# Three VectorE steps moved ahead of dE in a delta rule woven into a weight stream, and a 480-byte pad taken out

## The reference

```
proj = rms_norm(x) @ even_w_in        # attention A | qkv of B | gate z | beta, a
qkv  = silu(causal_conv(qkv_b));  q, k = l2_norm(q), l2_norm(k)
beta = sigmoid(beta_raw);  g = -exp(a_log) * softplus(a_raw + dt_bias)
# gated delta rule, 8 heads of 128, in chunks:
decay = exp(gam_i - gam_j) for i >= j             # gam = cumsum(g)
A     = I + strict_lower(beta_i * (k_i . k_j) * decay)
u, w  = solve(A, [v * beta, k * beta * exp(gam)])
v_new = u - w S
o     = (q exp(gam)) S + (q . k * decay, lower incl.) v_new
S     = S exp(gam_last) + (k exp(gam_last - gam))^T v_new
out_b = o * rsqrt(mean(o*o) + eps) * onorm * silu(z)
h     = x + concat(attention, out_b) @ even_w_out
```

## Time and profile before

| | |
|---|---|
| median of 3 runs | 2695.59 us (2693.42 to 2699.34) |
| the profiled execution, its time | 2695.59 us |
| its span, first to last instruction | 2693.8 us |
| TensorE busy | 2654.5 us, 99% |
| VectorE busy | 1548.3 us, 57% |
| ScalarE busy | 1263.1 us, 47% |
| mean granted TensorE clock | 0.998 of full |

### The profile page before, as it was taken

The page is one execution under the profiler, slowest core; times in us unless marked ns, Lnnn a source line. Parts: engine busy times, 40 slices in busy tenths (PEclk is TensorE's granted clock), DMA queues, the critical chain, the costliest instruction groups (busy, mean ns, idle before and its releaser), DMA issues.

```text
span 2693.8 us, 35362 instructions
## 1 busy us (share of the span) xinstructions
PE 2654.5 (99%) x12523; PEld 2206.6 (82%) x12523; DVE 1548.3 (57%) x2553; ACT 1263.1 (47%) x2381; POOL 28.6 (1%) x34
## 2 busy tenths in 40 slices
PE   8999999999999999999999999999999999999998
PEld 7778877888888888888788888888888888888876
DVE  6877756655555555555555555555555555565656
ACT  6552244544444444444555544444444444445433
POOL 1000000000000000000000000000000000000000
PEclk9999999999999999999999999999999999999999
DMA  7552223666565656557555656565656665565664
GB/s 220 176 161 86 66 92 110 194 181 196 185 194 187 190 187 193 190 193 227 165 171 188 198 181 198 182 195 186 194 186 192 192 190 155 172 180 171 178 233 158
DMA packets 251152, 477.47 MB, mean 177 GB/s; under 512 B 19080, under 2 KB 22912, under 8 KB 250400
## 3 DMA queue, kind: packets, MB, share of 16 engines
q1 hardware_dynamic: 245808, 467.92, 55.7%
q10 hardware_dynamic: 4656, 7.15, 0.7%
q0 software_dynamic: 576, 0.90, 0.1%
HBM read 473.82 MB, written 2.10 MB: 177 GB/s over the span
## 4 chain that ended last, share of the span: by engine, by line
PE 91%; DVE 6%; ACT 1%; issue 1%; DMA 0%; ACTq 0%; SPq 0%; POOL 0%; DVEq 0%
PE ps L1025 28%; PE ps L1027 28%; PE ps L1026 28%; PE ps L809 2%; DVE gs L1241 1%; DVE w_lo L1516 1%; PE ps L1088 1%; PE ps L1087 1%; ACT w_hi L711 0%; PE ps L1078 0%; DVE gs L1239 0%; PE ps L1167 0%; PE ps L1011 0%; PE ps L1009 0%; PE ps L1010 0%
## 5 line engine op out<-in xcount | busy, mean ns | idle before, releaser
L1516 DVE TENSOR_TENSOR w_lo<-raw,w_hi 128x512 fp32r<-128x512 f32 (+1 forms) x1776 | 1154.5, 686 | 745.9 <-ACT w_hi L711 743.2
L711 ACT CAST w_hi<-raw 128x512 fp32r<-128x512 f32 (+1 forms) x1776 | 1032.3, 622 | 708.9 <-PE ps L1027 567.8
L1025 PE MATMUL ps<-w_hi,xh 128*128 128x512 f32 (+1 forms) x2464 | 971.8, 394 | 7.8 <-DVE w_lo L1516 6.9
L1027 PE MATMUL ps<-w_hi,xl 128*128 128x512 f32 (+1 forms) x2464 | 957.5, 389 | 0.0
L1026 PE MATMUL ps<-w_lo,xh 128*128 128x512 f32 (+1 forms) x2464 | 956.4, 388 | 0.0
L1025 PEld LDWEIGHTS ps<-w_hi,xh 128*128 128x128 f32 x2464 | 463.4, 188 | 105.4 <-DVE w_lo L1516 15.4
L1027 PEld LDWEIGHTS ps<-w_hi,xl 128*128 128x128 f32 x2464 | 463.0, 188 | 96.6
L1026 PEld LDWEIGHTS ps<-w_lo,xh 128*128 128x128 f32 x2464 | 463.7, 188 | 90.0
L1025 PE MATMUL ps<-w_hi,fh 128*128 128x512 f32 x1056 | 416.3, 394 | 5.7 <-DVE w_lo L1516 5.7
L1027 PE MATMUL ps<-w_hi,fl 128*128 128x512 f32 x1056 | 412.4, 391 | 0.0
L1026 PE MATMUL ps<-w_lo,fh 128*128 128x512 f32 x1056 | 412.1, 390 | 0.0
(11 more groups left out here) (292 smaller groups left out, 1105.9 us busy)
## 6 DMA issues: line engine op xcount, KB each, us to landing
raw<-in_ffn_w_gate SPq DMA_DIRECT2D x176, 512.0 KB, 4.5
raw<-in_ffn_w_up SPq DMA_DIRECT2D x176, 512.0 KB, 4.6
raw<-in_ffn_w_down SPq DMA_DIRECT2D x176, 512.0 KB, 4.3
raw<-in_w_in SPq DMA_DIRECT2D x112, 512.0 KB, 4.1
raw<-in_even_w_in SPq DMA_DIRECT2D x80, 512.0 KB, 3.7
raw<-in_odd_w_in SPq DMA_DIRECT2D x64, 512.0 KB, 4.4
raw<-in_even_w_out SPq DMA_DIRECT2D x32, 512.0 KB, 3.8
raw<-in_odd_w_out SPq DMA_DIRECT2D x32, 512.0 KB, 4.6
```

The source lines that it names most:

```text
L711: act.copy(w_tile(w_hi, w2_hi, blk, k), raw[:, slot, kk, 0:blk.width]).then_inc(hi_ready, 1)
L1025: pe.matmul(acc(blk, t), hi_x[:, blk.kt0 + k, tok], hi_w, start=(k == 0), stop=False)
L1027: ins = pe.matmul(acc(blk, t), lo_x[:, blk.kt0 + k, tok], hi_w, start=False, stop=(k == blk.nk - 1))
L1516: TT(w_tile(w_lo, w2_lo, blk, k), raw[:, slot, kk, 0:w], w_tile(w_hi, w2_hi, blk, k).bitcast(F32), ALU.subtract).then_inc(lo_ready, 1)
```

## The change

What VectorE does in `delta()` stays the same; three pieces stand elsewhere in its queue. dD is made in step 3. The causal mask is put on dQK in step 4, before the product with the scores, which also moves there. At t = 1 o_ss is made in step 5. ScalarE's and TensorE's queues are unchanged. Beside this, the tensor `pad_x` of 120 floats per partition, used by nothing, is gone, so all that is laid out behind it stands 480 bytes lower.

```
-        sb("pad_x", [P, 120])
...
                         TT(dC[:, four, :], dL[:, four, :], each(masks[:, 0, :], 4), ALU.mult).then_inc(c_ready, 1)
                     yield
+                    dve.wait_ge(c_ready, 2 * t + 2)
+                    TT(dD[:, :, :], each(ident, 8), dC[:, :, :], ALU.subtract)
+                    yield
+                    link(TT(dQK[:, :, :], dQK[:, :, :], each(upper, 8), ALU.mult))
                     dve.wait_ge(kq_mm, 2 * t + 2)
                     TT(dQK[:, :, :], quarters(4, 2), dQK[:, :, :], ALU.mult).then_inc(lqk_ready, 1)
                     yield
-                    yield
+                    if t == 1:
+                        dve.wait_ge(o_sq, 1)
+                        link(dve.tensor_reduce(o_ss, v_new[:, :, :], AX.X, ALU.add))
+                        TS(o_ss, o_ss, 1.0 / B_HD, EPS, ALU.mult, ALU.add).then_inc(o_ms, 1)
                     yield
                     for half in range(2):
                         four = slice(4 * half, 4 * half + 4)
                         dve.wait_ge(de_mm, 2 * LEVELS * t + half + 1)
                         TT(dE[:, four, :], each(ident, 4), quarters(6 + half), ALU.subtract).then_inc(de_ready, 1)
-                    dve.wait_ge(c_ready, 2 * t + 2)
-                    TT(dD[:, :, :], each(ident, 8), dC[:, :, :], ALU.subtract)
                     yield
                     for lv in range(1, LEVELS):
                         if lv == 1:
                             dve.wait_ge(back_copied, 12)
                             TT(heads(vn[:, t, :]), heads(vn[:, t, :]), spread(beta[:, t, :], 8), ALU.mult)
-                            if t == 1:
-                                dve.wait_ge(o_sq, 1)
-                                link(dve.tensor_reduce(o_ss, v_new[:, :, :], AX.X, ALU.add))
-                                TS(o_ss, o_ss, 1.0 / B_HD, EPS, ALU.mult, ALU.add).then_inc(o_ms, 1)
...
-                        if lv == 3:
-                            dve.wait_ge(lqk_ready, 2 * t + 2)
-                            TT(dQK[:, :, :], dQK[:, :, :], each(upper, 8), ALU.mult)
```

## The result

The changed kernel takes 2760.93 us (median of four runs, 2759.05 to 2762.0) against 2694.57 us for the kernel before on the same chip: a ratio of 1.0242, 95% interval 1.0224 to 1.026. That is 66 us slower, where 4.75 were forecast. The profiled execution has a span of 2758.9 us.

A forecast was written before the change was run, and what follows sets the result against it. TensorE, busy in 99% of the span, was taken as the bound. Later L1087 starts and one clock fall, 1.47 + 1.58 + 1.7 = 4.75 us, on 2695.6 gave 2700.3 us; range 2692.5 to 2706.

The forecast's parts named there:

- pad_x removed: SBUF layout: tensors behind the pad start 32 bytes past a multiple of 512; effect on TensorE and VectorE taken as 0.
- the fourth rival: Alignment matters for 12,523 matmuls: one nanosecond each is 12.5 us, 2712.8 slower (chance 0.09) or 2687.8 faster (0.06).
- The 512 of the prediction: SBUF layout: with the pad, tensors behind it start on a multiple of 512 bytes; without it, 32 past one.
- the slower sign: Weight stream: removing the pad adds one nanosecond to each matmul, 12.5 us, 2712.8 us in all; chance 0.09.
- The moved steps: VectorE's queue before dE: dE 2.38 and 3.71 us later, L1087 1.47 (t=0) and 1.58 us (t=1) later.
- The waits theory: TensorE at 205 to 345 us, VectorE's order reversed: 4.3 us of waits shrink to 0.4, giving 2691.5 us.
- The clock: TensorE behind the new waits before L1078: one fall of the clock at t=1, 1.7 us; 0 at t=0.
- Covers: Weight tiles behind L1078: loads of raw issued 2 to 4 us later, counted 0, at most 3.7 us.

The follow-up runs named there:

- mask_back: Changed kernel with pad_x kept and the causal mask of dQK put back at level 3; 2697.83 us against 2695.2, ratio 1.001.
- the reverse edit: Kernel before, with vn * beta, o_ss and three later side products put behind dY in VectorE's queue; 2690.69 us against 2695.52, ratio 0.9987.

## Why the prediction was wrong, point by point

**The step that failed** is "pad_x removed": "So 0 for TensorE". It had the earlier trace rows for it: 275 ns for L1053 and for L1078. Both rows are of matmuls over 128 columns, not of the stream's 128x512 in fp32r, as the fourth rival said itself. And they were read for the wrong quantity. I asked where an operand starts, and took `extra` as the example of a bad start. The sum for the stream should have had 6.2 to 6.3 ns for each of its 10,560 matmuls, some 60 us. What the runs show is a matter of two operands: L1053 reads the same slice of `extra` as moving and as stationary tile, at a distance of 0, and so stood well by the rule found here. Its equal time was no evidence. L1058, with dqT and `extra`, stood 224 bytes over a multiple of 256 before and on one after, and takes the same (275 ns, and 112 from start to start, both times), so the effect was not seen in the small products at all, only in the stream. The prediction named the sign that came: it is wrong if the weight stream's matmuls have another mean.

The 512 of the prediction was worked out from the sizes of the tensors alone. The addresses are 128 past a multiple of 512, which changes nothing: the distance is what the pad sets.

**The rival with the right mechanism** was the fourth, with 0.09 for the slower sign. Its arithmetic holds (each nanosecond on each matmul), but it was given one nanosecond, and 2712.8 us; it measured 6.2 to 6.3. The two sides of that bound came from no row. An effect on the operation that is 10,560 times in the program, which no row showed at another distance, had no upper end, and the range should have said so, or the alignment been weighed by what it would cost.

**The moved steps** went as worked out. dE 3.71 us later at t=1 (3.71 forecast); from L1543 to dE at t=0 8.59 us against 6.20, 2.39 more (2.38 forecast). The waits before dE's product 1.72 to 1.87 and 3.94 to 4.08 us (1.8 to 2.0 and 4.1 forecast). Measured alone they cost 3.4 us (interval 0.8 to 5.7), with 4.75 forecast. The waits theory also gave 3.9 us for the reverse edit, which measured 4.8.

**The clock.** A fall came behind the 4 us wait in both profiled executions with all three steps moved. The Trainium skill ("TensorE: Matmul & The Clock Gate", HAM oscillation) leads one to expect that of gaps in which TensorE waits. This case's windows agree there, 0.70 in the changed kernel, but not at every gap: the clock stayed at 1.00 behind waits of 1.72, 1.96 and 2.83 us (changed kernel, kernel before, mask_back). The shorter wait at t=0 was followed by one fall in two executions. I had 0 there; the rows allowed either.

**Covers.** No new wait for w_lo appeared in the stretches, so the 0 for the delayed loads was right. And without the pad the first 455 us lost only 0.7 us, in part because slower matmuls shorten the waits for a late VectorE.

## What to carry to other kernels

Before an edit moves anything in SBUF, unused bytes too, work out the distance between the moving and the stationary tiles of the operation that fills the program, and keep it: here a multiple of 256 bytes is worth 2.2%. Compare the mean of that operation's rows first when a result doesn't fit; a change of 6 ns in 390 was nearly the whole answer, and a stretch in which both layouts occur in one execution showed it without a further run. An operation that TensorE doesn't wait for belongs behind the one it waits for in VectorE's queue, and counting start to start placed such waits to within 0.3 us here.

## What the runs showed of the hardware that was not expected

TensorE's matmuls of 128x512 in fp32r follow each other in 227 ns where the moving and the stationary tiles lie a multiple of 256 bytes apart in SBUF, and in 232.5 ns at a distance of 128 over one, 233.3 at 32, 64 and 224, and 234.2 at 96. With the distance kept, three different starts gave the same time (2694.91 and 2696.33 us against 2695.5). One tensor off slows the matmul in front of it too: 44.6 us for w_lo alone, 42 for w_hi, 40 for xh, and 60 for all. Products over 128 columns in plain float32 did not show it (L1058: 275 ns at 224 over a multiple and on one).
